# Attention stages of a two-block kernel: more spare PSUM banks for gate sums, dense products regrouped, weight roundings in two halves

## The chip, the cores and the metric

The kernel runs on one core of one Trainium2 chip. The metric is the device time of one execution in microseconds (us). Five engines work at the same time, each with its own instruction stream: PE (TensorE, matrix products), DVE (VectorE), ACT (ScalarE), POOL (GpSimd) and SP (which here only issues transfers). They meet at semaphores: an instruction waits until a counter has reached a number, and everything behind it in the same stream waits with it.

## The reference, cut to what matters

Two transformer-like blocks run one after the other on 512 tokens of width 1024, in fp32. The change touches the attention part of the first block:

- A projection `h @ w_in` gives queries, keys and values for two attentions and two wide gates, `gate_a` and `gate_b` (512 x 1024 each).
- The second attention (stick-breaking, 8 heads): `z = q k / 8`, `log_a = log_sigmoid(z) + sum of log_sigmoid(-z) over the keys between`, `o = exp(log_a) v` over strictly earlier keys.
- The first attention (sparse, 8 heads): an indexer scores all earlier keys, each token keeps its best 128 keys, and a softmax over these weighs the values.
- Merge: `merged = sigmoid(gate_a) * (y_a @ w_o_a) + sigmoid(gate_b) * (y_b @ w_o_b)`, then `x + merged @ w_out`.

The gates need only `h`, not the attentions, so their products can be computed at any time in between.

## The kernel before, in words

**Dense products.** A dense product in fp32 quality is made of three fp32r matmuls (`mm3`, lines 212 to 214): the weights are split into a rounded part `wh` and a rest `wl`, the activations likewise. Weights come in units of 128 x 2048 elements. SP loads a unit into `raw` (two slots), ACT rounds it to `wh` (line 192), POOL computes `wl` in two instructions (line 203) and then counts `w_lo` up, and PE waits for that count before the unit's first product. This is a fixed order of units through the whole kernel.

**Fillers.** In the attention stages PE would often wait for ACT, DVE and POOL. The kernel puts dense products of the merge into these gaps by hand. They are cut into 32 jobs: jobs 0 to 15 are the gate sums (8 `mm3` each, 512 columns, one PSUM bank each), jobs 16 to 23 are `y_b @ w_o_b`, 24 to 31 are `y_a @ w_o_a` (4 `mm3` each). `fill(pe, n)` (line 810) issues the next n `mm3` of this list wherever it is called; at a job's first product it puts the waits for the weights (`w_lo`) and for the PSUM bank. Two jobs of the gates share a weight unit, four of the others do.

**Banks.** PSUM has 8 banks of 512 fp32 columns. All gate jobs use bank 7, but jobs 10 and 12 use bank 5 (`SPARE`, line 783). A gate sum is copied out of its bank to `stage_b` or `stage_a` (`gate_copy`, line 853, done by ACT or DVE, counted in `fl_ev`), and SP stores it from there to DRAM; the gates come back later. So a job in bank 7 that follows one in bank 7 waits for the copy between.

**The stick-breaking stage** (`stick_pe`, line 1145) goes over four pairs of heads. For each pair PE computes scores into banks 0 to 5 (`pair_scores`), then fillers, then the output of the pair before (`stick_out`, bank 6), then fillers, then for each of the two heads the running sums (line 1161) which need the chain ACT (abs, exp, ln), DVE (softplus, line 1215), POOL (mask, line 958, counted in `b_spm`). The numbers of fillers at these four places are `STICK`; `AHEAD` stand before the first pair, `LATE` before the last `stick_out`. At the end of each pair ACT rounds the next weight unit and POOL computes its rest. DVE works off the top-k rounds of the indexer beside it.

**The sparse stage** (`sparse_pe`, line 1236) goes over 32 steps (4 blocks of queries x 8 heads) and some steps to drain. In step g PE computes scores of heads g and g+1 (even g only, line 1246, banks 0 and 1), `SPARSE[g]` fillers, every fourth step the values of four heads (line 1259, needs `pT`), and the transposes of the weights of step g-2 (line 1267, banks 2 to 5). In its iteration g ACT does the exp of step g (line 1282), scales step g-1 (`pr`, line 1288), after every fourth step copies the transposed weights out (`pT`, line 1294), and then, if a gate job ended in PE's step g, copies the gate (line 859) and, after every second job, rounds a whole weight unit. DVE adds the mask and takes the maximum (line 1315), which allows the scores two steps later (`a_lg`).

**After it** (`merge1_pe`) PE works off the rest of the jobs without a gap, and `w_out` follows.

The order in every stream is fixed by the code; nothing is planned at run time.

Of the kernel before, what the change touches and what calls it, by code (L numbers as in the profile page):

```python
# [22 lines left out]
ACT = mybir.ActivationFunctionType  # L23
# [4 lines left out]
NT = T // P  # L28
D = 1024
KD = D // P  # L30
# [18 lines left out]
def two_blocks_kernel(nc, A, out):  # L49
# [3 lines left out]
    def at(name, shape, dt=F32, offset=None):  # L53

        size = 4 * int(np.prod(shape[1:]))
        if offset is None:
            offset = sb_next[0]
            sb_next[0] += (size + 31) // 32 * 32
        assert offset + size <= 229368, (name, offset + size)
        return nc.alloc_sbuf_tensor_at(name, shape, dt, offset=offset)  # L60

    def sem(name):
        return nc.alloc_semaphore(name)


    raw = at("raw", [P, 2, 2048])
    wh = at("wh", [P, 2, 2048], F32R)
# [33 lines left out]
    n = 0  # L101
# [5 lines left out]
    w_in = [sem("w_in0"), sem("w_in1")]  # L107
    w_hi = sem("w_hi")
    w_lo = sem("w_lo")
    w_used = sem("w_used")  # L110
# [83 lines left out]
    def rounds(act, u, n, size=2048):  # L194
        for j in range(u, u + n):
            round_unit(act, j, j % 2, j // 2, size)
# [546 lines left out]
    def by_act(name):  # L743

        return m1_act, M1_ACT.index(name) + 1
# [7 lines left out]
    fl_mm, fl_ev = sem("fl_mm"), sem("fl_ev")  # L753
# [23 lines left out]

    um = U["merge1"]
    GATES, JOBS = 2 * KD, 4 * KD
    AHEAD, STICK, LATE = 4, (4, 6, 2, 4), 4  # L780
    SPARSE = 4 * [2, 1, 2, 1, 2] + 4 * [1, 1, 2] + [4, 4, 8, 4, 12]
    STEPS1 = [8 + AHEAD + 4 * sum(STICK) + LATE] + SPARSE
    SPARE = (10, 12)
    at_mm = {"n": 0}

    def products(j):

        return 8 if j < GATES else 4

    def unit_of(j):  # L790

        return um + (j // 2 if j < GATES else GATES // 2 + (j - GATES) // 4)

    def ends_unit(j):
        return j + 1 == JOBS or unit_of(j + 1) != unit_of(j)

    def bank_of(j):
        if j < GATES:
            return 5 if j in SPARE else 7
        return (7, 0, 1)[(j - GATES) % 3] if j < GATES + KD else 2 + (j - GATES - KD) % 5  # L800

    def job_done(j):

# [4 lines left out]
    def ended(step):  # L808

        a, b = sum(STEPS1[:step]), sum(STEPS1[:step + 1])  # L810
        ends = list(itertools.accumulate(products(j) for j in range(JOBS)))
        return [j for j in range(JOBS) if a < ends[j] <= b]

    def fill(pe, n):

        for _ in range(n):
            at_mm["n"] += 1
            ends = list(itertools.accumulate(products(j) for j in range(JOBS)))
            j = next(j for j in range(JOBS) if ends[j] >= at_mm["n"])
            k = at_mm["n"] - 1 - (ends[j] - products(j))  # L820
            u = unit_of(j)
            if k == 0:
                if j == 0 or ends_unit(j - 1):
                    pe.wait_ge(w_lo, u + 1)
                before = [i for i in range(min(j, GATES)) if bank_of(i) == bank_of(j)]
                if j <= GATES and before:
                    pe.wait_ge(fl_ev, before[-1] + 1)
                if j == GATES:
                    pe.wait_ge(b_lo, 4)
                if j == GATES + 1:  # L830
                    pe.wait_ge(a_lg, 8 * NT)
                if GATES + 3 <= j < GATES + KD:
                    pe.wait_ge(g_mul, j - GATES - 2)
                if j == GATES + KD:
                    pe.wait_ge(a_ylo, 8)
                if j >= GATES + KD + 5:
                    pe.wait_ge(g_mul, j - GATES - 4)
            if j < GATES:
                c, cols, mh, ml = j % 2, HALF, h_hi, h_lo
            else:  # L840
                c, cols, (mh, ml) = j % 4, 512, ((yb_hi, yb_lo) if j < GATES + KD else (ya_hi, ya_lo))
            at_k = slice(k * cols + c * P, k * cols + (c + 1) * P)
            ins = mm3(PS[:, bank_of(j), :], wh[:, u % 2, at_k], wl[:, u % 2, at_k], mh[:, k, :], ml[:, k, :],
                      k == 0, k == products(j) - 1)
            if k == products(j) - 1:
                if ends_unit(j):
                    ins.then_inc(w_used, 1)
                else:
                    ins.then_inc(fl_mm, 1)
# [11 lines left out]
    def gate_out(act, step):  # L861

        for j in ended(step):
            if 10 <= j < GATES:
                gate_copy(act, act_copy, j)
                if ends_unit(j):
                    rounds(act, unit_of(j) + 2, 1)

    def merge1_sp(sp):
        w = A['w_in'][0]  # L870
# [270 lines left out]
    def stick_pe(pe):  # L1141

        fill(pe, AHEAD)
        pe.wait_ge(a_relu, 8 * (NT - 1))
        pe.wait_ge(*by_act("vb"))
        pe.wait_ge(qb_set, 1)
        for p in range(4):
            if p:
                pe.wait_ge(b_exp, 2 * p)
            pair_scores(pe, p, kbT, qbT, b_z)  # L1150
            fill(pe, STICK[0])
            if p:
                stick_out(pe, p - 1)
            fill(pe, STICK[1])
            for h in (2 * p, 2 * p + 1):
                z = scores_of(h)
                pe.wait_ge(b_spm, h + 1)
                for j in range(NT):
                    for i in range(j, NT):
                        c = off[j] + (i - j) * P  # L1160
                        ins = nc.tensor.matmul(z[:, c:c + wid[i]], negtri[:, :] if i == j else negone[:, :],  # L1161
                                               stick[:, h % 3, off[i]:off[i] + wid[i]], start=False, stop=i == NT - 1,
                                               skip_group_check=True)
                ins.then_inc(b_acc, 1)
                fill(pe, STICK[2 + h % 2])
        fill(pe, LATE)
        stick_out(pe, 3)

    def stick_out(pe, p):

        pe.wait_ge(b_am, 2 * p + 2)
        if p:
            pe.wait_ge(b_lo, p)
        for j in range(NT):
            for h in (2 * p, 2 * p + 1):
                r = PER * (h % 2)
                ins = nc.tensor.matmul(PS[r:r + PER, 6, j * P:T], vb[:, j, h * PER:(h + 1) * PER],
                                       stick[:, h % 3, off[j]:off[j] + wid[j]], start=j == 0, stop=j == NT - 1,
                                       skip_group_check=True)
        ins.then_inc(b_pv, 1)  # L1180
# [55 lines left out]
    def sparse_pe(pe):  # L1236
        pe.wait_ge(b_exp, 8)
        for g in range(GS + LAG + 3):
            if g < GS:
                if g % 2 == 0:  # L1240
                    i, S = g // 8, (g // 8 + 1) * P
                    if g:
                        pe.wait_ge(a_lg, g)
                    for h in (g % 8, g % 8 + 1):
                        r = PER * (h % 2)
                        nc.tensor.matmul(PS[:, h % 2, 0:S], qaT[r:r + PER, h // 2, i * P:(i + 1) * P],
                                         kaT[r:r + PER, 0:S], start=True, stop=True).then_inc(a_lgm, 1)
            fill(pe, SPARSE[g])
            n = g - LAG
            if n >= 4 and n % 4 == 0:  # L1250
                quad = n // 4 - 1
                tiles_seen = quad // 2 + 1
                pe.wait_ge(a_pTev, quad + 1)
                pe.wait_ge(a_ylo, quad) if quad else pe.wait_ge(b_lo, 4)
                for pair in range(2):
                    for j in range(tiles_seen):
                        for h in (2 * pair, 2 * pair + 1):
                            r, v = PER * (h % 2), (4 * (quad % 2) + h) * PER
                            ins = nc.tensor.matmul(PS[r:r + 64, 6, pair * P:(pair + 1) * P], pn[:, j, v:v + PER],  # L1259
                                                   pT[:, j, h * P:(h + 1) * P], start=j == 0, stop=j == tiles_seen - 1,  # L1260
                                                   skip_group_check=True)
                ins.then_inc(a_o, 1)
            if 0 <= n < GS:
                i, h = n // 8, n % 8
                pe.wait_ge(a_pr, n + 1)
                for j in range(i + 1):
                    ins = pe.transpose(PS[:, 2 + j, (h % 4) * P:(h % 4 + 1) * P], pr[:, n % 3, j * P:(j + 1) * P], ident[:, :])
                ins.then_inc(a_pT, 1)
# [1481 lines left out]
```

## Time and profile before

| | us |
|---|---|
| median of 3 runs (lowest, highest) | 2224.5 (2224.17, 2225.02) |
| the profiled execution | 2225.48 |
| its span, first to last instruction | 2223.8 |
| PE busy in the span | 2196.0 (99%) |
| ACT busy | 814.2 (37%) |
| DVE busy | 1037.6 (47%) |
| POOL busy | 930.9 (42%) |

The mean granted clock of TensorE is 0.999 of full speed. The chain of work that ended last is 95% PE. Times of single instructions are told from the span's start; the stretch of the change lies between 491 and 741 us. In a timeline a row gives the start, the duration, the engine, the line of the kernel, the instruction with what it writes and reads, and in brackets how long the engine was idle before it and who released it. Matmuls overlap: their durations are longer than the distance from one start to the next, so what a matmul costs is read from starts.

### The profile page before, as it was taken

What the parts mean: (1) busy time and instruction counts of PE and PEld (TensorE: products, weight loads), DVE (VectorE), ACT (ScalarE), POOL (GpSimd) and SP (SyncE); (2) the same over time, 40 slices, a digit from 0 to 9 for tenths busy, and PEclk for the clock granted to TensorE, in tenths of its full rate; (3) what the DMA queues carried; (4) which work ended last, traced back from release to release, by engine and by line L of the source; (5) the groups of instructions that cost most, each with busy time, mean ns of one, the idle gap of its engine ahead of it and who ended that gap; (6) DMA issues with size and microseconds to landing.
All of it is one profiled execution on the core that took longest, in us unless ns stands there. A gap on an engine that the chain in (4) does not pass through costs nothing.

```text
span 2223.8 us, 30107 instructions
## 1 busy us (share of the span) xinstructions
PE 2196.0 (99%) x12142; PEld 1780.9 (80%) x12142; DVE 1037.6 (47%) x1471; ACT 814.2 (37%) x864; POOL 930.9 (42%) x513
## 2 busy tenths in 40 slices
PE   8999999999999999999999999999999999999998
PEld 6888888776767888888888788888888878888887
DVE  5433202655843353331045441747566546888701
ACT  4222313537666332222143542333334244222212
POOL 4555444342332445555444244423233243444343
PEclk9999999999999999999999999999999999999999
DMA  4333323253333333322233123313121243332223
GB/s 155 95 95 94 95 94 113 79 79 50 69 119 105 95 102 102 98 85 95 98 102 95 58 76 95 96 39 96 58 77 57 93 145 105 95 95 94 69 94 112
DMA packets 162444, 203.93 MB, mean 92 GB/s; under 512 B 12260, under 2 KB 117031, under 8 KB 162343
## 3 DMA queue, kind: packets, MB, share of 16 engines
q1 hardware_dynamic: 155584, 197.69, 29.4%
q10 hardware_dynamic: 6759, 4.80, 0.7%
q8 instruction: 75, 1.23, 0.2%
q14 instruction: 26, 0.21, 0.0%
HBM read 191.97 MB, written 10.49 MB: 91 GB/s over the span
## 4 chain that ended last, share of the span: by engine, by line
PE 95%; ACT 2%; DVE 1%; POOL 0%; issue 0%; DMA 0%; SPq 0%; POOLq 0%; ACTq 0%; DVEq 0%
PE PS L212 24%; PE PS L214 24%; PE PS L213 24%; PE PS L243 2%; PE PS L245 2%; PE PS L244 2%; PE PS L2529 2%; PE PS L2530 2%; PE PS L2531 2%; PE PS L1161 1%; PE PS L2181 1%; PE PS L1698 1%; PE PS L2198 1%; PE PS L1077 1%; PE PS L1259 0%
## 5 line engine op out<-in xcount | busy, mean ns | idle before, releaser
L203 POOL TENSOR_TENSOR wl<-raw,wh 128x1024 fp32r<-128x1024 f32 x335 | 854.7, 2567 | 1189.8 <-ACT wh L192 1189.8
L212 PE MATMUL PS<-h_hi,wh 128*128 128x512 f32 x1696 | 677.0, 399 | 3.9 <-ACT stage_a L859 1.5
L214 PE MATMUL PS<-h_hi,wl 128*128 128x512 f32 x1696 | 661.2, 390 | 0.0
L213 PE MATMUL PS<-h_lo,wh 128*128 128x512 f32 x1696 | 660.7, 390 | 0.0
L192 ACT ACTIVATE wh<-raw 128x2048 fp32r<-128x2048 f32 (+1 forms) x214 | 332.6, 1554 | 826.3 <-PE PS L214 708.9
L212 PEld LDWEIGHTS PS<-h_hi,wh 128*128 128x128 f32 x1696 | 318.5, 188 | 87.3 <-issue 17.5
L214 PEld LDWEIGHTS PS<-h_hi,wl 128*128 128x128 f32 x1696 | 318.3, 188 | 67.5
L213 PEld LDWEIGHTS PS<-h_lo,wh 128*128 128x128 f32 x1696 | 318.8, 188 | 62.0 <-issue 1.0
L689 DVE SCALAR_TENSOR_TENSOR xT<-PS,xT 128x512 f32<-128x512 f32 x32 | 21.8, 688 | 283.8 <-PE PS L214 283.8
L572 DVE TENSOR_TENSOR act_lo<-work,act_hi 128x1024 f32 (+1 forms) x33 | 64.3, 1949 | 179.6 <-ACT act_hi L519 179.6
L212 PE MATMUL PS<-act_hi,wh 128*128 (+1 forms) x352 | 137.2, 390 | 0.0
L214 PE MATMUL PS<-act_hi,wl 128*128 (+1 forms) x352 | 137.0, 389 | 0.0
L213 PE MATMUL PS<-act_lo,wh 128*128 (+1 forms) x352 | 136.9, 389 | 0.0
L212 PEld LDWEIGHTS PS<-act_hi,wh 128*128 128x128 f32 x352 | 66.1, 188 | 14.5 <-issue 0.8
L214 PEld LDWEIGHTS PS<-act_hi,wl 128*128 128x128 f32 x352 | 66.1, 188 | 13.9
L213 PEld LDWEIGHTS PS<-act_lo,wh 128*128 128x128 f32 x352 | 66.1, 188 | 13.7
L243 PE MATMUL PS<-wh,h_hi 128*128 128x512 f32 x192 | 75.9, 395 | 0.0
L557 DVE TENSOR_TENSOR work<-PS,norm 128x1024 f32<-128x1024 f32 x22 | 26.9, 1224 | 104.5 <-PE PS L214 104.5
L245 PE MATMUL PS<-wh,h_lo 128*128 128x512 f32 x192 | 74.8, 390 | 0.0
L244 PE MATMUL PS<-wl,h_hi 128*128 128x512 f32 x192 | 74.7, 389 | 0.0
L2529 PE MATMUL PS<-wh,act_hi 128*128 128x512 f32 x176 | 68.7, 391 | 1.0 <-POOL wl L203 1.0
L2531 PE MATMUL PS<-wh,act_lo 128*128 128x512 f32 x176 | 68.5, 389 | 0.0
(453 smaller groups left out, 3054.5 us busy)
## 6 DMA issues: line engine op xcount, KB each, us to landing
raw<-in_w_in_dram SPq DMA_DIRECT2D x94, 512.0 KB, 4.6
raw<-in_w_up_dram SPq DMA_DIRECT2D x82, 512.0 KB, 4.7
raw<-in_w_down_dram SPq DMA_DIRECT2D x132, 256.0 KB, 2.7
raw<-in_w_gate_dram SPq DMA_DIRECT2D x42, 512.0 KB, 3.8
raw<-in_w_in_dram SPq DMA_DIRECT2D x20, 256.0 KB, 3.8
raw<-in_w_out_dram SPq DMA_DIRECT2D x16, 256.0 KB, 2.8
raw<-in_w_ret_br_dram SPq DMA_DIRECT2D x8, 512.0 KB, 4.3
gates<-stage SPq DMA_DIRECT2D x16, 256.0 KB, 5.5
```

Of the source, the lines that this page charges most:

```text
L192: nc.scalar.activation(wh[:, slot, 0:size], raw[:, slot, 0:size], ACT.Copy).then_inc(w_hi, 1)
L203: ins = nc.gpsimd.tensor_tensor(wl[:, slot, part], raw[:, slot, part], wh[:, slot, part].bitcast(F32), ALU.subtract)
L212: nc.tensor.matmul(dst, sh, mh, start=start, stop=False)
L213: nc.tensor.matmul(dst, sh, ml, start=False, stop=False)
L214: return nc.tensor.matmul(dst, sl, mh, start=False, stop=stop)
L243: nc.tensor.matmul(dst, a, W[:, k, :], start=first and k == 0, stop=False)
L244: nc.tensor.matmul(dst, a, L[:, k, :], start=False, stop=False)
L245: ins = nc.tensor.matmul(dst, b, W[:, k, :], start=False, stop=last and k == nk - 1)
L572: dve.tensor_tensor(act_lo[:, bass.ds(2 * j, 2), :], src, act_hi[:, bass.ds(2 * j, 2), :].bitcast(F32), ALU.subtract).then_inc(a_ready, 1)
L2529: nc.tensor.matmul(dst, a, w, start=False, stop=False, skip_group_check=True)
L2530: nc.tensor.matmul(dst, a, l, start=False, stop=False, skip_group_check=True)
L2531: return nc.tensor.matmul(dst, b, w, start=False, stop=stop, skip_group_check=True)
```

## The change

- `STICK` gets its own four numbers for each pair of heads: (4, 8, 2, 4) for the first, (2, 8, 2, 4) for the others, in place of (4, 6, 2, 4) for all. `LATE` is 2 in place of 4. The sum is the same (72 with `AHEAD`).
- `SPARSE` of steps 20 to 31 becomes 2,1,2,1,2,1,1,2,1,1,1,1 in place of four times 1,1,2. The sum is the same (16); job 14 ends in step 24 in place of 25, job 15 in step 31 as before.
- Job 2 goes to bank 6 and job 14 to bank 5. The first `stick_out` waits for three gate copies (bank 6), and the first transposes of the last query block wait for 15 (bank 5).
- The `y_b` jobs use banks 0, 1, 7 in turn in place of 7, 0, 1. Job 16 waits for the last mask of the sparse stage (`a_lg`) in place of the copy of job 15; job 18 waits for that copy.
- In the sparse stage the rounding of a 128 x 2048 unit is done as two ACT instructions of 128 x 1024: one in the iteration as before, the other in the next one. The count `w_hi` goes up after the second.

```diff
@@ -777,10 +777,10 @@
-    AHEAD, STICK, LATE = 4, (4, 6, 2, 4), 4
-    SPARSE = 4 * [2, 1, 2, 1, 2] + 4 * [1, 1, 2] + [4, 4, 8, 4, 12]
-    STEPS1 = [8 + AHEAD + 4 * sum(STICK) + LATE] + SPARSE
-    SPARE = (10, 12)
+    AHEAD, STICK, LATE = 4, ((4, 8, 2, 4), (2, 8, 2, 4), (2, 8, 2, 4), (2, 8, 2, 4)), 2
+    SPARSE = 4 * [2, 1, 2, 1, 2] + [2, 1, 2, 1, 2, 1, 1, 2, 1, 1, 1, 1] + [4, 4, 8, 4, 12]
+    STEPS1 = [8 + AHEAD + sum(sum(s) for s in STICK) + LATE] + SPARSE
+    SPARE = {2: 6, 10: 5, 12: 5, 14: 5}
@@ -796,8 +796,8 @@
         if j < GATES:
-            return 5 if j in SPARE else 7
-        return (7, 0, 1)[(j - GATES) % 3] if j < GATES + KD else 2 + (j - GATES - KD) % 5
+            return SPARE.get(j, 7)
+        return (0, 1, 7)[(j - GATES) % 3] if j < GATES + KD else 2 + (j - GATES - KD) % 5
@@ -823,12 +823,13 @@
-                if j <= GATES and before:
+                if j < GATES and before:
                     pe.wait_ge(fl_ev, before[-1] + 1)
                 if j == GATES:
                     pe.wait_ge(b_lo, 4)
-                if j == GATES + 1:
                     pe.wait_ge(a_lg, 8 * NT)
+                if j == GATES + 2:
+                    pe.wait_ge(fl_ev, GATES)
@@ -864,7 +865,20 @@
                 if ends_unit(j):
-                    rounds(act, unit_of(j) + 2, 1)
+                    half_round(act, unit_of(j) + 2, 0)
+        for j in ended(step - 1):
+            if 10 <= j < GATES and ends_unit(j):
+                half_round(act, unit_of(j) + 2, 1)
+
+    def half_round(act, u, half):
+
+        part = slice(1024 * half, 1024 * half + 1024)
+        if half == 0:
+            act.wait_ge(w_in[u % 2], 32 * (u // 2 + 1))
+            act.wait_ge(w_used, u - 1)
+        ins = act.activation(wh[:, u % 2, part], raw[:, u % 2, part], ACT.Copy)
+        if half:
+            ins.then_inc(w_hi, 1)
@@ -1148,10 +1162,10 @@
-            fill(pe, STICK[0])
+            fill(pe, STICK[p][0])
             if p:
                 stick_out(pe, p - 1)
-            fill(pe, STICK[1])
+            fill(pe, STICK[p][1])
@@ -1162,13 +1176,15 @@
-                fill(pe, STICK[2 + h % 2])
+                fill(pe, STICK[p][2 + h % 2])
         fill(pe, LATE)
         stick_out(pe, 3)
     def stick_out(pe, p):
         pe.wait_ge(b_am, 2 * p + 2)
+        if p == 0:
+            pe.wait_ge(fl_ev, 3)
@@ -1263,6 +1279,8 @@
                 pe.wait_ge(a_pr, n + 1)
+                if n == 8 * (NT - 1):
+                    pe.wait_ge(fl_ev, 15)
```

## Rows read from the trace of the kernel before

**Rows 1.** Stretch, length, busy of PE, PEld, DVE, ACT, POOL (count), clock, DMA, GB/s.
```profile
513.50:618.20 104.70, 102.31 (x493) 72.75 (x492) 72.47 (x161) 74.30 (x62) 39.82 (x74) 1.00 0.34 61
618.20:701.00 82.80, 79.85 (x498) 56.15 (x496) 31.48 (x143) 60.86 (x125) 19.12 (x9) 1.00 0.39 123
```

**Rows 2.** All waits of PE from 470 to 760: total us, times, longest.
```profile
PE PS L1161 <- POOL work L958: 1.5, 2, 1.1
PE PS L212 <- ACT stage_a L859: 1.5, 1, 1.5
PE PS L212 <- DVE stage_b L856: 0.9, 1, 0.9
PE PS L212 <- issue: 0.6, 1, 0.6
PE PS L1267 <- ACT pr L1288: 0.5, 1, 0.5
PE PS L212 <- POOL wl L203: 0.5, 1, 0.5
PE PS L1259 <- ACT pT L1294: 0.4, 1, 0.4
```

**Rows 3.** Timeline of PE, first pair of heads: start, duration, line, instruction, idle before.
```profile
518.49 0.39 PE L214 MATMUL PS<-h_hi,wl 128*128 128x512 f32 x1
519.75 0.47 PE L212 MATMUL PS<-h_hi,wh 128*128 128x512 f32 x1 [0.87 <-DVE stage_b L856]
...
525.17 1.12 PE L1161 MATMUL PS<-work,negtri 128*128 128x512 f32 x2 [1.05 <-POOL work L958]
...
531.62 1.12 PE L1161 MATMUL PS<-work,negtri 128*128 128x512 f32 x2 [0.46 <-POOL work L958]
```

**Rows 4.** Timeline of PE at the end of the stick-breaking stage.
```profile
614.45 0.39 PE L212 MATMUL PS<-h_hi,wh 128*128 128x512 f32 x1
...
615.13 0.39 PE L212 MATMUL PS<-h_hi,wh 128*128 128x512 f32 x1
...
615.90 2.37 PE L1177 MATMUL PS<-work,vb 128*64 128x512 f32 x16
...
618.63 0.50 PE L212 MATMUL PS<-h_hi,wh 128*128 128x512 f32 x1
```

**Rows 5.** Timelines of POOL, SP's queue and DVE at the same place.
```profile
613.65 4.72 POOL L203 TENSOR_TENSOR wl<-raw,wh 128x1024 fp32r<-128x1024 f32 x2 [0.79 <-ACT wh L192]
...
618.40 0.93 SPq L140 DMA_DIRECT2D raw<-in_w_in_dram  x2
...
620.69 0.15 DVE L1317 TENSOR_SCALAR rstat<-rstat 128x1 f32<-128x1 f32 x1
```

**Rows 6.** Timeline of PE in the sparse stage: the four places where it waited.
```profile
659.04 0.55 PE L1267 MATMUL PS<-ident,pr 128*128 128x128 f32 x3 [0.53 <-ACT pr L1288]
...
671.50 0.50 PE L212 MATMUL PS<-h_hi,wh 128*128 128x512 f32 x1 [1.47 <-ACT stage_a L859]
...
682.23 1.97 PE L1259 MATMUL PS<-pT,pn 128*64 128x128 f32 x32 [0.39 <-ACT pT L1294]
...
687.16 0.47 PE L212 MATMUL PS<-yb_hi,wh 128*128 128x512 f32 x1 [0.56 <-issue]
```

**Rows 7.** Timeline of ACT in the sparse stage: rounding, exp, scaling, pT, gate copy.
```profile
655.99 1.91 ACT L192 ACTIVATE wh<-raw 128x2048 fp32r<-128x2048 f32 x1
...
668.23 0.71 ACT L1282 ACTIVATE pr<-lg,rstat 128x512 f32<-128x512 f32 x1
...
669.54 1.43 ACT L1294 ACTIVATE pT<-PS 128x1536 f32<-128x1536 f32 x1
...
670.87 0.58 ACT L859 ACTIVATE stage_a<-PS 128x512 f32<-128x512 f32 x1
...
680.32 1.86 ACT L1294 ACTIVATE pT<-PS 128x2048 f32<-128x2048 f32 x1
```

**Rows 8.** Timeline of ACT in the merge: a rounding of 1024 columns.
```profile
727.98 1.05 ACT L192 ACTIVATE wh<-raw 128x1024 fp32r<-128x1024 f32 x1
```

## The prediction

> **What bounds the kernel now.** I read the page first. PE is busy 99% of the span and the chain that ended last is 95% PE, so only what shortens PE's own stream or removes its waits can move the end. The change neither adds nor removes a PE instruction: the fillers of each stage keep their sum. So the whole gain has to come out of PE's waits in the stretch it touches, and the list of these waits comes next [rows 2]: seven kinds, 5.9 us together, of which 0.5 us (POOL `wl` after 735 us, in `w_out`) lies behind the change. The two stages themselves take 104.7 and 82.8 us at a granted clock of 1.00, with ACT busy for 74.3 and 60.9 us [rows 1]; PE is the fullest engine in both, but ACT is second and feeds PE.
>
> Then the timelines, to price each wait. Two fillers lie 0.68 us apart [rows 4], so one matmul costs 0.23 us, while its row lasts 0.39 us. A wait therefore costs the idle time shown plus 0.16 us, the part of the last matmul that the next one would have overlapped. In the stick-breaking stage that makes 0.87 + 0.16 = 1.03 us (bank 7, copy of job 1), 1.05 + 0.16 = 1.21 us and 0.46 + 0.16 = 0.62 us (masks of the first two heads): 2.86 us [rows 3]. In the sparse stage 0.69 us (`pr`), 1.63 us (copy of job 14), 0.55 us (`pT`) and 0.72 us (the start of job 16, shown as "issue"; what it waits for is the copy of job 15 in bank 7): 3.59 us [rows 6]. All of it: 6.45 us. This is the ceiling of any gain.
>
> **First pair of heads, job 2 to bank 6.** The 1.03 us at 519.75 goes, since bank 6 has no earlier gate sum. What is late next is the mask of the first head, which lets PE go on at 525.17 [rows 3]. That chain (ACT, DVE, POOL) starts from scores that PE has finished before these fillers, so it ends at 525.17 in both kernels. PE just does 8 fillers instead of 6 until then: from 518.49 + 0.23 = 518.72, 8 x 0.685 = 5.48 us, to 524.2, still 1 us early. So no time is won here, but two products (1.37 us) are done ahead. The second mask at 531.62 stays as it is. Job 2's weights are not late: in the trace job 2 was released by the copy, not by `wl`.
>
> **The other pairs: 2, 8 in place of 4, 6.** The output of the pair before moves ahead by two products, 1.37 us. The job after it starts 1.37 us earlier too, and needs the weight unit that POOL finishes after each pair. In the last pair that is 8.1 us after the end of the running sums (8 fillers before 615.90, so 610.3, to 618.40 [rows 4, 5]). In the middle pairs PE has 4 fillers (2.74), the scores (16 matmuls like `stick_out`, so I take its 2.37 us), 2 fillers (1.37) and `stick_out` (2.37) before that job: 8.9 us. The weights are 0.8 us early and I take 0; if the scores were much shorter, PE would wait for POOL for a few tenths in three pairs.
>
> **LATE 2, and the first sparse filler.** The two products done ahead are now missing before the last `stick_out`: it starts at 615.90 - 1.37 = 614.53, and job 10's first product would come at 618.63 - 1.37 = 617.26 [rows 4]. But job 10 opens a new weight unit. POOL works on it from 613.65 to 618.37, behind ACT's rounding after the last exp of the stage, and SP's next load, which waits for the same count, is issued at 618.40 [rows 5]. PE can't start job 10 before 618.42. So 1.16 of the 1.37 us turn into a wait for POOL. The remaining 0.2 us are lost as well: the scores of step 2 need DVE's maximum of step 1, which ends at 620.84 [rows 5], and PE issued them at 620.91 before, with three products from 618.63 on. DVE comes from the top-k rounds and doesn't get earlier. So the whole stick-breaking part is worth 0, at best 0.2 us.
>
> **Sparse stage, steps 0 to 19.** Same fillers. The rounding after job 11 is halved; that moves ACT's exps by some tenths where PE has no wait in the list of row size. I take 0 (0 to 0.2 us).
>
> **Step 20 and the halves.** At 659.04 PE waited for `pr` [rows 6], because a rounding of 1.91 us from 655.99 stood in front of it on ACT [rows 7]. A half lasts 1.05 us [rows 8], so exp and `pr` come up to 0.9 us sooner; and step 20 has one product more, so PE comes 0.68 us later to this place. The 0.69 us wait is thus filled by a product. PE stands at 659.04 again, one product ahead. The second half costs ACT 2 x 1.05 - 1.91 = 0.2 us more in all and sits in front of the next exp; the next `pT` is then about 0.6 us later and meets PE at about the moment it is needed (0 to 0.2 us of wait).
>
> [...]
>
> **Job 14 to bank 5, job 15 without its wait.** The 1.63 us at 671.50 go. Without them the product of step 26 starts at 671.50 - 1.63 = 669.87 and the values behind it would be due 0.9 us later, at 670.8. They need `pT`, on ACT from 669.54 to 670.97 [rows 7]. But job 14 now ends in step 24, so its copy (0.58 us) stands before the exp at 668.23 instead of behind `pT`: `pT` runs from 670.1 to 671.55. The values start at 671.6 instead of 671.50 + 0.91 = 672.4. Of 1.63 us, 0.8 is won and 0.8 is a new wait for ACT.
>
> At the next values (682.23 before, with `pT` from 680.32 [rows 6, 7]) the same chain rules: scores go out 0.8 us earlier, step 27 has a product more and step 28 one less, so `pT` comes 0.6 to 0.7 us earlier. PE goes on at about 681.6: 0.63 us earlier, and still one product ahead.
>
> **Job 16 in bank 0.** Step 31 has one product instead of two, so the product done ahead in step 20 is cashed: 0.68 us. The 0.72 us at 687.16 go, since the new wait, DVE's maximum of step 31, lies before the values at 682 and is long past. What it cost if it were late: nothing else is queued behind it but the tail of the sparse stage. Job 18, which now has the wait for the copy, comes 8 products later.
>
> **Sum.** Job 16 starts 0.63 + 0.68 + 0.72 = 2.03 us earlier. From there PE runs without a wait through 32 products to `w_out`, and its weights, copies and sums follow PE; the 0.5 us wait there moves along. 2225.48 - 2.0 = 2223.5 for the profiled execution. The median of the runs lies 0.98 us below that execution; the forecast on it is 2224.5 - 2.0 = 2222.5. Bounds: if each half and the copy cost ACT once more on the way to both `pT` (0.58 + 0.2 us), 1.2 is left; if neither `pT` makes PE wait (0.8 + 0.7 + 0.2), 3.7.
>
> **Rivals.**
>
> *ACT takes it all.* The waits for banks go, but every later `pT` is as late as PE used to be, so only job 16's 0.72 us remain at most. For: ACT is the second engine in this stage, and both `pT` already end within 0.1 us of PE's need. Against: ACT still idles a quarter of the stage [rows 1]. 2224.5 - 0.4 = 2224.1.
>
> *Everything is covered.* No `pT` and no `pr` is waited for, PE runs from 659 to job 16 without a break: 3.7 us, 2220.8. For: the fillers now stand in front of the two waits. Against: the copy of job 14 moves in front of an exp that `pT` depends on.
>
> *Slower: ACT becomes the bound of steps 24 to 31.* One step of ACT is exp 0.71, `pr` about 0.7, a quarter of `pT` (1.86 / 4) and of the small copies: 2.0 us [rows 7]. PE's step there with one product is 2.17 us: steps 26 to 31 take 15.66 us from 671.50 to 687.16, less the two waits (1.27) and two of the eight products (1.37), by 6 [rows 6]. If a half and a copy, each with its handover, push ACT's step above 2.2 us, each of the 8 steps loses the excess, and from 0.25 us on that eats the gain; at 0.35 us it is 8 x 0.35 = 2.8 us: 2225.3. For: steps 28 to 31 now have one product each, so PE asks for the next `pr` with little in between. Against: only one copy and one half fall into these steps.
>
> *No effect:* the waits at 671.50 and 687.16 were not the bank's. The copy of job 14 ends at 670.87 + 0.58 = 671.45, 0.05 us before PE goes on [rows 6, 7], so this is hard to hold. 2224.5.
>
> **How the numbers follow.** Forecast (1.2 to 3 us gained) 0.60; ACT takes it 0.18; all covered 0.09; slower 0.07; no effect 0.06. The range 2220.5 to 2224.6 reaches from all covered to no effect; left out are the slower case and 0.05 on either side for what the rows don't show, 0.17 in all. A measurement of this kernel tells about 0.2% (4.45 us) from no change. Faster by more than that would need over two thirds of all 6.45 us of waits, while the masks (1.8 us) and POOL's unit (1.2 us) stay by the working above: 0.05. Slower by 4.45 us would need the slower case at 0.8 us a step: 0.03. Within: 0.92.
>
> **What would show it.** Right: no wait of PE for `stage_a` or `stage_b`; a new one of about 1.2 us for POOL `wl` at 617 to 618.5; the masks' waits as before (the first near 0.8 us idle); waits for `pT` of about 0.6 us each near 671 and 681; job 16 at about 685.1. Wrong: job 10 starting before 618 (then `LATE` is worth 1 us more), no waits for `pT`, or waits for `pr` in several steps after 667, which is the slower case.

## The result and the profile after

The changed kernel takes 2230.09 us (median of 11 executions, 2228.67 to 2233.12), the kernel before 2224.75 us beside it (11 executions, 2224.17 to 2226.05). The ratio is 1.0025, 95% interval 1.0018 to 1.0033: slower by 5.3 us. The forecast was 2222.5, the range 2220.5 to 2224.6, and slower by over 0.2% had a chance of 0.03. The prediction was wrong.

The profiled execution of after took 2233.12 us, the slowest of the eleven, 7.64 us more than that of before (2225.48). First the engines, on the page:

```profile
PE 2199.3 (99%) x12142; PEld 1783.1 (80%) x12142; DVE 1038.8 (47%) x1471; ACT 813.9 (36%) x867; POOL 931.5 (42%) x513
```

PE is still 99% busy; the share says nothing about a loss of 0.3%. Then all waits of PE from 470 to 760 us, as in [rows 2]: total us, times, longest.

```profile
PE PS L212 <- ACT stage_b L860: 5.4, 3, 1.8
PE PS L212 <- POOL wl L203: 1.8, 2, 1.2
PE PS L1175 <- POOL work L972: 1.3, 2, 0.9
PE PS L1275 <- ACT pT L1312: 1.0, 2, 0.6
PE PS L1285 <- ACT pr L1306: 0.4, 1, 0.4
```

Most of this was foreseen: the waits for `stage_a`, for the DVE copy and the "issue" of job 16 are gone, POOL `wl` and two `pT` waits have come. The first line was not: three waits of 1.8 us for a gate copy into `stage_b`. Where they lie, in PE's timeline (these places answer to [rows 3, 4, 6]; the timeline of after starts this stage 0.33 us earlier, as the scores of the first pair show, 513.18 against 513.51):

```profile
524.84 1.12 PE L1175 MATMUL PS<-work,negtri 128*128 128x512 f32 x2 [0.85 <-POOL work L972]
...
554.52 0.39 PE L1175 MATMUL PS<-work,negtri 128*128 128x128 f32 x2
556.72 0.50 PE L212 MATMUL PS<-h_hi,wh 128*128 128x512 f32 x1 [1.81 <-ACT stage_b L860]
...
585.21 0.50 PE L212 MATMUL PS<-h_hi,wh 128*128 128x512 f32 x1 [1.81 <-ACT stage_b L860]
...
612.02 0.50 PE L212 MATMUL PS<-h_hi,wh 128*128 128x512 f32 x1 [1.81 <-ACT stage_b L860]
...
627.73 0.50 PE L212 MATMUL PS<-h_hi,wh 128*128 128x512 f32 x1 [1.25 <-POOL wl L203]
...
680.61 1.53 PE L1275 MATMUL PS<-pT,pn 128*64 128x128 f32 x24 [0.55 <-ACT pT L1312]
...
688.04 0.66 PE L1285 MATMUL PS<-ident,pr 128*128 128x128 f32 x4 [0.41 <-ACT pr L1306]
...
691.12 1.97 PE L1275 MATMUL PS<-pT,pn 128*64 128x128 f32 x32 [0.47 <-ACT pT L1312]
...
694.56 0.47 PE L212 MATMUL PS<-yb_hi,wh 128*128 128x512 f32 x1
```

The three waits stand behind the running sums of the first head of pairs 2, 3 and 4. Eight fillers before these sums finish job 4 (6, 8), so the product behind them opens job 5 (7, 9) in the same bank 7 and needs the copy of job 4. In the first pair the eight fillers are job 2, which has bank 6 to itself, so job 3 behind the sums finds bank 7 free. From the start of the last sum to the next product it is 2.20 us (554.52 to 556.72) in place of 0.14 us at the same place before (554.83 to 554.97), so each wait costs 2.06 us, 6.18 us in all. Why the copy is late is seen on ACT:

```profile
553.18 1.28 ACT L1211 ACT_TABLE_LOAD   x1
554.94 1.24 ACT L1211 ACTIVATE work<-PS 128x1280 f32<-128x1280 f32 x1 [0.47 <-PE PS L1175]
556.08 0.59 ACT L860 ACTIVATE stage_b<-PS 128x512 f32<-128x512 f32 x1
```

ACT's order is exp of the first head, then the gate copy. The exp needs the very sums that PE has just finished; PE's next product needs the copy behind the exp. So each engine waits for the other, once in each of the last three pairs.

That explains 6.2 us. The scores, which open each pair, show what else there is. Timelines of PE, all four pairs in after, then the last three in before:

```profile
513.18 2.43 PE L1151 MATMUL PS<-qbT,kbT 64*128 64x512 f32 x16
...
538.59 2.43 PE L1151 MATMUL PS<-qbT,kbT 64*128 64x512 f32 x16
...
567.08 2.43 PE L1151 MATMUL PS<-qbT,kbT 64*128 64x512 f32 x16
...
593.89 2.43 PE L1151 MATMUL PS<-qbT,kbT 64*128 64x512 f32 x16
```

```profile
538.90 2.43 PE L1137 MATMUL PS<-qbT,kbT 64*128 64x512 f32 x16
...
563.66 2.43 PE L1137 MATMUL PS<-qbT,kbT 64*128 64x512 f32 x16
...
588.42 2.43 PE L1137 MATMUL PS<-qbT,kbT 64*128 64x512 f32 x16
```

Before, the pairs lay 24.76 us apart. After, the step from the third pair to the fourth is 26.81 us, 2.05 more: the wait. That from the second to the third is 28.49 us, and there another 1.68 us are lost in which PE waits for nobody. The stretches behind the three waits (start and end, length, busy of PE, PEld, DVE, ACT, POOL with counts, granted clock, DMA share, GB/s):

```profile
557.50:561.50 4.00, 4.00 (x9) 2.16 (x8) 3.79 (x10) 0.00 (x0) 0.00 (x0) 0.57 0.23 83
...
586.00:590.00 4.00, 4.00 (x17) 2.75 (x16) 3.77 (x10) 0.00 (x0) 0.00 (x0) 1.00 0.21 70
...
612.50:616.00 3.50, 3.50 (x9) 2.04 (x8) 3.33 (x9) 0.00 (x0) 0.07 (x1) 0.51 0.20 77
```

PE is fully busy in all three, but in the first and the last the granted clock is near the lower level (0.50 of 2.4 GHz): in 4 us PE gets 9 matmuls done in place of 17, and this lasts some 3 us. Behind the second wait, which was as long, the clock stayed at 1.00. So in this execution 3 x 2.06 + 2 x 1.7 = 9.6 us are lost in the stick-breaking part, and the sparse part gives 1.7 us back: from job 10 to job 16 it takes 66.83 us (627.73 to 694.56) against 68.53 (618.63 to 687.16 [rows 4, 6]). 9.6 - 1.7 = 7.9, against 7.64 measured.

### The profile page after: what moved, and what is told of

The parts are those of the page before. It is cut to its first block, busy times and chain, and to the rows that moved or that the text cites. A ratio compares the mean times of both kernels' runs of the same rounds, so it can differ in the third digit from the quotient of the medians.

```text
span 2231.4 us, 30111 instructions
## 1 busy us (share of the span) xinstructions
PE 2199.3 (99%) x12142; PEld 1783.1 (80%) x12142; DVE 1038.8 (47%) x1471; ACT 813.9 (36%) x867; POOL 931.5 (42%) x513
## 4 chain that ended last, share of the span: by engine, by line
PE 95%; ACT 2%; DVE 1%; POOL 1%; issue 1%; DMA 0%; ACTq 0%; POOLq 0%; DVEq 0%
PE PS L212 24%; PE PS L214 23%; PE PS L213 23%; PE PS L243 2%; PE PS L244 2%; PE PS L245 2%; PE PS L2547 2%; PE PS L2549 2%; PE PS L2548 2%; PE PS L1175 1%; PE PS L2199 1%; PE PS L1716 1%; PE PS L2216 1%; POOL wl L203 1%; PE PS L1091 1%
## 5 line engine op out<-in xcount | busy, mean ns | idle before, releaser
L192 ACT ACTIVATE wh<-raw 128x2048 fp32r<-128x2048 f32 (+1 forms) x211 | 326.9, 1549 | 824.0 <-PE PS L214 706.6
```

The costliest lines, as they stand in the source:

```text
L192: nc.scalar.activation(wh[:, slot, 0:size], raw[:, slot, 0:size], ACT.Copy).then_inc(w_hi, 1)
```

## The experiments

Theory: the fillers' new order puts each bank-7 handover of three pairs behind an exp on ACT. Rivals: the sparse stage (halved roundings, new rhythm, banks) is what costs, or job 2 and bank 6. All kernels were timed beside the kernel before, which had medians of 2224.53 to 2224.95. Of each run one execution is profiled. Where traces of two kernels are compared, distances within a trace are used, or times from the scores of the first pair, since the traces start this stage up to 1.1 us apart.

**1. The fillers of before, everything else of after.**

```diff
-    AHEAD, STICK, LATE = 4, ((4, 8, 2, 4), (2, 8, 2, 4), (2, 8, 2, 4), (2, 8, 2, 4)), 2
+    AHEAD, STICK, LATE = 4, 4 * ((4, 6, 2, 4),), 4
```

> The changed kernel with the four filler counts of the stick-breaking stage as before (4, 6, 2, 4 in every pair, LATE 4); bank 6 for job 2, the new rhythm of the sparse stage, its banks and the halves stay. Theory W: the time was lost in three waits of PE of 2.06 us each, for ACT's copy of jobs 4, 6 and 8, because 8 fillers in place of 6 put the first product of jobs 5, 7 and 9 right behind the running sums of a pair's first head; each such wait can be followed by a stretch at granted clock 0.50 (1.7 us each, two of them in the profiled execution). The sparse part itself wins 1.7 us. So here: no wait for stage_b, no stretch below clock 0.99, and 2224.75 - 1.7 = 2223.0 (2222.5 to 2223.5). Rival S: the sparse part (halves, new rhythm) is what costs, then 2226 or more. Rival C: the stretches at half clock come with the new rhythm and not from the waits, then they are seen here too: 2223.0 + 0.8 to 1.7, so 2223.8 to 2224.7, with granted clock 0.998 in some executions.

Measured: 2223.75 us (2222.55 to 2224.32), ratio 0.9993 (0.9984 to 1.0002). PE's waits have no `stage_b`; the first mask, with two fillers less ahead of it, now shows 2.2 us:

```profile
PE PS L1175 <- POOL work L972: 2.7, 2, 2.2
PE PS L1275 <- ACT pT L1312: 1.0, 2, 0.6
...
```

So the loss is the fillers'. The rest of the change wins 1.2 us by the medians, if anything: the interval reaches 1. In the traces it is 1.70 us: from the first scores to job 16 PE needs 171.95 us in place of 173.65. The median lies above the 2222.5 to 2223.5 expected. Five of the eleven executions list a mean clock of 0.998, and all five took 2223.61 us or more; the three at 1.000 took 2223.22 or less. So a low clock seems to cost time in some executions of this kernel too, as rival C has it, though no wait for `stage_b` is left. The profiled one is among the three (1.00 from 490 to 740 us), so where it falls is open; the first mask's 2.2 us is the longest wait in the stretch of the change.

**2. The fillers of after (and job 2 in bank 6 with its wait), nothing else.**

```diff
-    AHEAD, STICK, LATE = 4, (4, 6, 2, 4), 4
+    AHEAD, STICK, LATE = 4, ((4, 8, 2, 4), (2, 8, 2, 4), (2, 8, 2, 4), (2, 8, 2, 4)), 2
...
-    SPARE = (10, 12)
+    SPARE = {2: 6, 10: 5, 12: 5}
```

> The kernel before with only the new filler counts of the stick-breaking stage (and bank 6 for job 2 with its wait); the sparse stage is as before. Theory W: three waits of 2.06 us, so 2224.75 + 6.2 = 2230.9 without a stretch at half clock, 2232.6 with one, 2234.3 with two; median 2231 to 2233. The sparse stage then shows its old waits (0.5, 1.5, 0.4, 0.6 us idle). Rival S: 2224 to 2226. Rival C (the clock falls by the rhythm of the sparse part): 2230.9 and no stretch at half clock.

Measured: 2231.92 us (2230.06 to 2232.29), ratio 1.0031 (1.002 to 1.0043). The new wait and the old ones of the sparse stage stand side by side:

```profile
PE PS L212 <- ACT stage_b L859: 5.4, 3, 1.8
PE PS L212 <- POOL wl L203: 1.6, 2, 1.1
PE PS L212 <- ACT stage_a L859: 1.5, 1, 1.5
...
```

The one part alone brings the whole loss, within the 2231 to 2233 expected; the rival of the sparse stage falls. The profiled execution (2230.38 us) has no stretch at half clock behind any of its three waits.

**3. After, with ACT's gate copy ahead of the pair's two exps.** The fillers stay as in after; only the place of one copy per pair in ACT's stream moves.

```diff
+            act.wait_ge(fl_ev, 2 * p + 2)
+            gate_copy(act, act_copy, 2 * p + 2)
             for h in (2 * p, 2 * p + 1):
                 act.wait_ge(b_acc, h + 1)
                 act.activation(stick[:, h % 3, :], scores_of(h), ACT.Exp).then_inc(b_exp, 1)
-                if h % 2 == 0:
-                    gate_copy(act, act_copy, 2 * p + 2)
```

> The changed kernel, but ACT copies the gate sum of jobs 2, 4, 6, 8 ahead of the two exps of the pair (behind the last ln) instead of behind the first exp; nothing else moves. Theory W: the copy is done about when the running sums end, so the three waits fall from 2.06 us to 0 to 0.2 us; the exp of the first head comes some 0.1 to 0.6 us later, which nothing on PE waits for. No stretch at half clock. 2224.75 - 1.7 = 2223.0 (2222.7 to 2223.7). Rival P: jobs 5, 7 and 9 really waited for something else (weights of POOL), then the waits stay and the time is 2229 to 2232. Rival C: the clock still falls, 2223.8 to 2225.

Measured: 2222.72 us (2222.44 to 2223.52), ratio 0.999 (0.9981 to 0.9999), at the lower end of what was expected and 0.2 us from the prediction's 2222.5, and no `stage_b` wait. ACT at the same place:

```profile
552.38 0.58 ACT L860 ACTIVATE stage_b<-PS 128x512 f32<-128x512 f32 x1
552.97 1.28 ACT L1213 ACT_TABLE_LOAD   x1
554.27 1.24 ACT L1213 ACTIVATE work<-PS 128x1280 f32<-128x1280 f32 x1
```

The copy is done at 552.96, while PE still works on the sums. The wait is the copy's place, not the bank and not the number of fillers. By the lowest executions of the first run of after and of this one (2228.67 and 2222.44) the place is worth 6.2 us, the sum of the three waits.

**4. A smaller dose: two products between the sums and job 5.**

```diff
-    AHEAD, STICK, LATE = 4, ((4, 8, 2, 4), (2, 8, 2, 4), (2, 8, 2, 4), (2, 8, 2, 4)), 2
+    AHEAD, STICK, LATE = 4, ((4, 8, 2, 4), (2, 6, 4, 4), (2, 6, 4, 4), (2, 6, 4, 4)), 2
```

> The changed kernel with 2, 6, 4, 4 fillers in the last three pairs in place of 2, 8, 2, 4: two more products stand between the running sums of the first head and the first product of jobs 5, 7, 9. Theory W: the waits shrink by two products (1.37 us), from 2.06 to 0.69 us each, so 2224.75 - 1.7 + 2.1 = 2225.1 (2224.6 to 2225.6) if a wait of that size brings no stretch at half clock; with one stretch 1.7 more. Rival S: within 1 us of the changed kernel's 2230.1.

Measured: 2227.37 us (2226.83 to 2227.85), ratio 1.0011 (1.0002 to 1.002). The direction is right, the size is not: the waits show 1.28 us each, 1.44 us with the overlap, and the pairs lie 26.35 us apart against 24.73 in experiment 3, so each wait costs about 1.6 us, not 0.69. PE and ACT at the first of them:

```profile
552.35 0.39 PE L1175 MATMUL PS<-work,negtri 128*128 128x128 f32 x2
...
555.41 0.50 PE L212 MATMUL PS<-h_hi,wh 128*128 128x512 f32 x1 [1.28 <-ACT stage_b L860]
```

```profile
552.34 1.28 ACT L1211 ACT_TABLE_LOAD   x1
553.64 1.24 ACT L1211 ACTIVATE work<-PS 128x1280 f32<-128x1280 f32 x1
554.77 0.59 ACT L860 ACTIVATE stage_b<-PS 128x512 f32<-128x512 f32 x1
```

PE starts the last sum 1.36 us earlier than with 8 fillers (from the first scores), but ACT's exp doesn't follow: the load of its table ends only at 553.62. The exp starts 1.29 us after the last sum, not 0.42 us as in after. ACT's own stream takes 0.87 us of this back; I had let it follow PE.

**5 to 7. The parts of the sparse stage, on top of experiment 3**: the whole rounding (e5), the fillers' old rhythm (e6), and both (e9), which leaves only the banks.

```diff
-                    half_round(act, unit_of(j) + 2, 0)
...
+                    rounds(act, unit_of(j) + 2, 1)
```

```diff
-    SPARSE = 4 * [2, 1, 2, 1, 2] + [2, 1, 2, 1, 2, 1, 1, 2, 1, 1, 1, 1] + [4, 4, 8, 4, 12]
+    SPARSE = 4 * [2, 1, 2, 1, 2] + 4 * [1, 1, 2] + [4, 4, 8, 4, 12]
```

> The kernel with the copy ahead of the exps (e3, 2222.7 us), but in the sparse stage each weight unit is rounded in one instruction of 2048 columns as before the change. Theory W: the halves matter little: the wait for pr of step 19 is covered by the second product of step 20 either way (the whole rounding makes pr 0.4 us later than the half, the product gives 0.69 us), and the half that moved into the next iteration no longer delays the next pT by 0.6 us. 2222.7 (2222.2 to 2223.2). Rival H: the halves are what the sparse part wins by; without them 2223.6 or more.

> The kernel with the copy ahead of the exps (e3, 2222.7 us), but steps 20 to 31 have the old numbers of fillers (1, 1, 2 four times); banks and halves stay. Theory W, by the terms of the prediction: the banks alone remove the wait of 1.6 us for job 14's copy and of 0.7 us at job 16, but the product that was done ahead in step 20 is missing, so the wait for pr at step 19 comes back in part (0.3 us with the half) and 0.7 us of it is lost: 2223.2 to 2223.9. Rival R: the rhythm is what matters and the banks alone win nothing: 2224.3 or more.

> The kernel with the copy ahead of the exps (e3, 2222.7 us), with both the old numbers of fillers in steps 20 to 31 and the whole rounding: of the sparse part only the banks are left (job 14 in bank 5, jobs 16 to 18 in banks 0, 1, 7). Theory B: the banks win all of the sparse part, the halves and the rhythm replace each other at the wait for pr (either covers it, and the old rhythm with the halves left 0.17 us of it). Without both, that wait is 0.5 to 0.7 us again: e6 (2222.4) + 0.4 = 2222.8 (2222.3 to 2223.3). Rival T: it takes one of the two, and without both the next pT is late as well: 2223.5 or more.

Measured: 2222.77 us (2222.41 to 2224.23) with the whole rounding, 2222.38 (2221.55 to 2223.8) with the old rhythm, 2222.16 (2221.82 to 2224.59) with the banks alone; ratios 0.9992 (0.9983 to 1.0001), 0.999 (0.9981 to 0.9999), 0.9989 (0.998 to 0.9998). These intervals overlap, so the traces decide. From the first product of job 10 to that of job 16: 66.95 us in experiment 3 (617.32 to 684.27), 66.88 with the whole rounding, 66.45 with the old rhythm (617.44 to 683.89), 66.39 with the banks alone (617.60 to 683.99), 68.53 before. The other traces agree: with the new banks it is 66.80 to 66.95 us in all traces with the new rhythm, 66.39 to 66.45 in all with the old. So the banks win 2.1 us, the halves nothing in either rhythm (0.07 and 0.06 us more), and the new rhythm costs 0.5 us. The whole rounding came as expected; the expectations for the old rhythm (2223.2 to 2223.9) and for the banks alone (2222.3 to 2223.3) were both too high. PE's waits with the banks alone:

```profile
...
PE PS L1282 <- ACT pr L1303: 0.5, 1, 0.5
PE PS L1272 <- ACT pT L1309: 0.4, 1, 0.4
```

These two are the old waits of [rows 6]; no second `pT` wait has come. With job 14 ending in step 25 its copy stays behind `pT`. From the `pr` wait to the `pT` wait PE needs 21.80 us in place of 23.19, so 1.4 of the 1.63 us of job 14's bank are won, and from there to job 16 4.13 in place of 4.93, 0.8 us. In the old rhythm the halves only move a wait: `pr` falls from 0.53 to 0.17 us idle, and a `pT` wait of 0.41 us comes 3.4 us behind it. The new rhythm's waits add up to 1.43 us idle (`pT` 0.56 and 0.47, `pr` 0.40), the banks alone leave 0.94.

**8. A longer wait.** After, with the gate copies of jobs 4, 6 and 8 done three times in a row; nothing is left out.

```diff
                 if h % 2 == 0:
+                    if p:
...
+                        for _ in range(2):
+                            act_link(act_copy(stage_b[:, 0, :], PS[:, bank_of(2 * p + 2), :]))
                     gate_copy(act, act_copy, 2 * p + 2)
```

> The changed kernel, but ACT copies jobs 4, 6 and 8 three times one after the other, so that PE's three waits grow by two copies with their handover, about 1.4 us each, from 2.06 to about 3.5 us. Nothing is computed differently. If a stretch at half clock is what follows a long wait of PE, the dose goes up: 2228.8 (the changed kernel's executions without such a stretch) + 4.2 = 2233.0, and 1.7 us more for each stretch; with one in every pair 2238. If the stretches have nothing to do with the length of the wait, 2230.1 + 4.2 = 2234.3 and the same spread as the changed kernel (4.5 us).

Measured: 2237.22 us (2234.91 to 2238.14), ratio 1.0057 (1.0043 to 1.007). The waits grow to 3.07 us each, 3 x 1.26 = 3.8 us more, and the executions lie 2.2 to 5.4 us above 2222.7 + 6.2 + 3.8 = 2232.7, which fits one to three stretches at half clock of 1.7 us. The profiled one, the fastest, shows one, behind the second wait (which ended at 586.16):

```profile
PE PS L212 <- ACT stage_b L860: 9.2, 3, 3.1
...
```

```profile
558.00:561.00 3.00, 2.92 (x10) 1.99 (x11) 2.85 (x7) 0.02 (x1) 0.00 (x0) 1.00 0.25 90
...
588.00:590.00 2.00, 2.00 (x3) 0.80 (x3) 1.90 (x5) 0.00 (x0) 0.00 (x0) 0.50 0.03 7
```

The first row lies behind the first wait; behind the third (615 to 619 us) the clock is 1.00 too. So even 3.07 us of idling do not always bring the lower clock.

**9. The same waits without idling.** After, with seven throwaway matmuls into bank 6 at the three places.

```diff
                 ins.then_inc(b_acc, 1)
+                if p and h % 2 == 0:
+                    pe.wait_ge(b_lo, p)
+                    for _ in range(7):
+                        nc.tensor.matmul(PS[:, 6, :], h_hi[:, 0, 0:P], h_hi[:, 0, :], start=True, stop=True)
```

> The kernel after, with seven throwaway matmuls of 128x512 into bank 6 (free there) after the running sums of the first head of pairs 2, 3 and 4. They fill 7 x 0.23 = 1.6 us of the 2.06 us that PE loses at each of the three waits for ACT's gate copy, so PE waits as long for the copy but hardly idles. Theory (the half clock follows PE's idling at these three places): the waits shrink to 0.2 to 0.4 us idle, the loss of 6.2 us stays, no stretch at half clock is left: 2222.7 + 6.2 = 2228.9 us, all executions within 1.3 us of each other, clock 0.999 or 1.0. Rival (the half clock comes from something else in these stages, as the copy, the transfers or DVE's work): the same three groups as the kernel after, 2228.9, 2230.4 and 2232.5, median about 2230.1. A third way: the throwaway matmuls come late or take longer and hold up the first product: above 2229.5 with a small spread.

Measured: 2229.8 us, all eleven executions within 0.87 us (2229.44 to 2230.31); ratio 1.0023 (1.0014 to 1.0032). It is the third way for the size: the wait for DVE's `yb_lo` in front of them delays the matmuls, and they now set the delay themselves: the pairs lie 27.14 us apart against 24.73 in experiment 3, 2.4 us each in place of 2.1.

```profile
554.48 0.39 PE L1175 MATMUL PS<-work,negtri 128*128 128x128 f32 x2
555.38 1.90 PE L1182 MATMUL PS<-h_hi 128*128 128x512 f32 x7 [0.51 <-DVE yb_lo L1239]
557.12 0.40 PE L212 MATMUL PS<-h_hi,wh 128*128 128x512 f32 x1
```

For the clock it is the theory: PE loses at least as long as in after, but idles 0.51 us instead of 1.81, both steps between pairs are equal, the clock is 1.00 in each of the microseconds read behind the three places (556 to 563, 584 to 592, 611 to 618), all eleven list a mean clock of 0.999 or 1.000, and the groups of times are gone.

**10. After once more, for a second profile.** No edit.

> The kernel after, unchanged, beside the one with throwaway matmuls on the same chip, for a second profile of it. Theory: 2230.1 us median, executions in groups near 2228.9, 2230.4 and 2232.5, and the profiled one shows as many stretches at half clock as its time says: none at 2228.9, one at 2230.4, two at 2232.5; its three waits for ACT's gate copy are 1.81 us idle in any case. Rival (the groups come from another place in the kernel): the number of stretches at half clock between 550 and 620 us doesn't go with the time.

Measured: 2230.49 us (2228.38 to 2232.14), ratio 1.0025 (1.0016 to 1.0034). The profiled execution took 2230.51 us, in the middle group, and has one stretch at half clock, behind the second wait (which ended at 583.19):

```profile
584.00:585.00 1.00, 1.00 (x4) 0.72 (x4) 0.93 (x4) 0.00 (x0) 0.00 (x0) 0.50 0.76 262
...
587.00:588.00 1.00, 1.00 (x4) 0.61 (x3) 0.93 (x4) 0.00 (x0) 0.00 (x0) 0.88 0.01 4
```

The pairs are 26.82 and 28.45 us apart there (scores at 538.25, 565.07 and 593.52), in the reverse order of the first profile. Over both runs the 22 executions of after fall into three groups: 8 from 2228.38 to 2229.47, 9 from 2230.08 to 2230.82, 5 from 2232.1 to 2233.12. The two profiles, one stretch at 2230.51 and two at 2233.12, fit the upper two groups; that the lowest has none is concluded from its time. Not all of the spread need come from these three places: in experiment 12 below, which has no such wait, two of eleven executions list 0.998 and took 2222.45 and 2222.55 us, some 1.5 us above the median, and the kernel before has such executions too (2226.32 and 2226.72, beside a median of 2224.59). None of these was profiled.

**11 and 12. Better versions.** Experiment 3, with the last pair's weight unit rounded between its two exps, POOL's half of the rest between the masks, and DVE's top-k rounds shared out 15, 13, 11, 9 over the pairs (e8); and that with the old rhythm (e10).

```diff
                 earlier_keys(pool, h).then_inc(b_am, 1)
-            los(pool, um + 2 + p, 1)
+                if h == 6:
+                    pool.wait_ge(w_hi, um + 6)
+                    lo_half(pool, um + 5, 0)
...
+                if h == 6:
+                    rounds(act, um + 5, 1)
...
-        share = 3 * (TOPK // 8) // 4
+        share = (0, 15, 28, 39, 48)
```

> The kernel with the copy ahead of the exps (e3, 2222.7 us), and against the wait of 1.25 us for job 10's weights: in the last pair ACT rounds that unit between the two exps, POOL computes half of its rest between the two masks, so it is ready about 3 us earlier; DVE's 48 top-k rounds are dealt out 15, 13, 11, 9 over the pairs in place of 12 each, so that the first mask of the sparse stage isn't held up by them. Theory W: the wait at job 10 goes and nothing takes its place before the waits for pT: 2222.7 - 1.2 = 2221.5 (2221.0 to 2222.2). Rival D: DVE comes no earlier or a gate copy on DVE behind more top-k rounds becomes the next wait of PE: 2222.5 or more.

> The kernel of e8 (2221.6 us) with the old numbers of fillers in steps 20 to 31, which in e6 came out 0.3 us below the new ones. If that difference is real and adds up: 2221.2 (2220.8 to 2221.7), with waits for pT of 0.4 us each and for pr of 0.2 us as in e6. If it was noise: 2221.6 to 2222.

Measured: 2221.58 us (2221.28 to 2223.13), ratio 0.9987 (0.9978 to 0.9996), and 2220.99 us (2220.28 to 2222.55), ratio 0.9984 (0.9975 to 0.9993). Both lie where they were expected. The last is the best of all: 3.6 us under the kernel before. POOL's two halves in it end at 614.40, 3.2 us earlier from the first scores than before (618.37 [rows 5]):

```profile
607.12 2.36 POOL L977 TENSOR_TENSOR wl<-raw,wh 128x1024 fp32r<-128x1024 f32 x1 [0.78 <-ACT wh L192]
611.02 1.03 POOL L983 TENSOR_SCALAR_AFFINE_SELECT work<-work 128x128 f32<-128x128 f32 x4 [1.54 <-ACT work L1224]
612.01 2.39 POOL L977 TENSOR_TENSOR wl<-raw,wh 128x1024 fp32r<-128x1024 f32 x1
```

Job 10 starts without a wait at 616.45, from the first scores 1.15 us before that of experiment 6, which waits 1.08 us idle there. POOL's order and DVE's shares were changed together; what DVE's part is worth by itself no run shows.

## Why the prediction was wrong

**The step that failed** is "The other pairs: 2, 8 in place of 4, 6". It says that the job behind `stick_out` needs POOL's weights, finds 0.8 us of slack and takes 0. It treats only the job boundary in front of `stick_out`, which stays there and comes 1.37 us earlier. The regrouping moves another one: job 4 (6, 8), which ended two fillers behind the first head's sums before, now ends with the eighth filler ahead of them, job 5 (7, 9) opens right behind them, and its bank is released by a copy that stands behind an exp which waits for those sums. That is 3 x 2.06 us (experiments 2 and 3), and on top two stretches of 1.7 us at half clock in one profile and one in the other (experiments 9 and 10). In the slower rival the mechanism was another (ACT's step in the sparse stage); of its sign, waits for `pr` in several steps, a single one of 0.41 us is seen. The ceiling of 6.45 us held for the waits that were there, but says nothing of new ones; each boundary that moved had to be asked for its releaser.

**First pair: right.** The copy's wait is gone and the mask still decides: PE goes on 11.66 us after the first scores in both kernels (513.18 to 524.84, 513.51 to 525.17).

**LATE and job 10: right.** From the start of the last `stick_out` to job 10 it is 2.73 us before, 4.04 in after and 3.89 in experiment 3, so POOL's unit costs 1.31 and 1.16 us; 1.16 were worked out. In experiment 3 job 10 comes 0.29 us earlier from the first scores than before, where 0 to 0.2 were forecast. The better version confirms it from the other side: with POOL early, 1.1 us comes.

**Step 20 and the halves: wrong, a null term.** The `pr` wait at step 20 did go, but the product done ahead there is not cashed. The rhythm that gives it also moves job 14's copy in front of an exp and delays `pT`, and late in the stage there is a `pr` wait of 0.41 us at 688.04 that I had not foreseen. In sum the new rhythm costs 0.5 us where I had it win 0.68. The halves are worth nothing in time (2222.72 against 2222.77 us). On ACT the halves behind job 13 took 1.05 and 1.04 us against 1.91 for a whole one [rows 7], 0.18 us more:

```profile
664.97 1.05 ACT L879 ACTIVATE wh<-raw 128x1024 fp32r<-128x1024 f32 x1
...
667.51 1.04 ACT L879 ACTIVATE wh<-raw 128x1024 fp32r<-128x1024 f32 x1
```

The Trainium skill ("ScalarE: Activation LUTs", What ACT_TABLE_LOAD costs) gives an ACTIVATE with immediate scale and bias a fixed 186 ns beside 0.833 ns per element. The trace agrees, with 0.18 us for the one more.

**Job 14 and job 15: right in kind.** `stage_a` and the "issue" are gone, and the new `pT` waits are 0.55 and 0.47 us idle where about 0.6 each were forecast.

**The sum of the sparse stage: 1.7 us won, 2.03 forecast.** The term that is off is the rhythm's; the banks alone bring 2.1. Without the failing step the forecast would have stood: experiment 3 measures 2222.72. Its trace has job 16 1.87 us earlier from the first scores, 1.6 from the sparse part and 0.3 from the stick-breaking part, so the sum stands partly because two small misses go opposite ways.

## What to carry to other kernels

When work is moved between fill places, list every job boundary before and after the move, and for each the releaser of its buffer and what stands ahead of that releaser in its own engine's stream; a copy behind an instruction that waits for the consumer makes both engines wait. A wait of the bounding engine can cost more than its length, as the clock can fall after it (here 1.7 us on top of 2.06, in some executions). When an engine is moved earlier, its partner's stream does not move along: read what the partner still has to do first.

## What the runs showed of the hardware

- After three of the nine waits of 1.8 us that were profiled (three each in the two profiles of after and in experiment 2) the granted clock fell to 0.50 some 0.5 to 1.2 us after PE had resumed, for some 3 us, and cost 1.7 us; after the others it stayed at 1.00. Filled with throwaway matmuls to 0.51 us of idling, the same delays brought no fall in the profile and no sign of one in the times of eleven executions. After waits of 3.07 us it fell once in three. What decides between the two cases is left open.
- A gate copy of 128x512 on ACT lasts 0.59 us in after, and PE goes on 0.64 us after its start (556.08 to 556.72, and 554.77 to 555.41 in experiment 4). What makes the handover dear is what stands ahead of the copy.
